# Five fences between the stages of an encoder block, and the place of the merge's buffers

## The chip, the cores and the metric

The kernel runs on all 8 cores of one Trainium2 chip. Each core computes one element of the batch by itself; there is no exchange between cores. The metric is the device time of the slowest core, in microseconds (us).

TensorE multiplies matrices into PSUM (8 banks of 128 x 512 f32), VectorE (DVE), ScalarE (ACT) and GpSimd (POOL) read and write SBUF, and SyncE (SP) and GpSimd issue the loads. Each engine runs its own instructions in order and waits for the others by semaphores.

## The reference, cut to what matters

One layer on x of 2048 tokens x 1024 channels (each core's share), with f32 inputs:

```
x = x + 0.5 * swiglu(rmsnorm(x), ...)                  # D_FF = 2816
h = rmsnorm(x)
proj = h @ w_in        # q, k, v of NA | q (2 maps), k (2 maps), v of diff | q of memory
y_na   = neighbourhood_attention(...) @ w_br_na        # 8 heads of 64, window 8 x 16 on a 32 x 64 grid
y_diff = rmsnorm(differential_attention(...)) @ w_br_diff   # 4 heads, softmax1 - lam * softmax2
y_mem  = memory_attention(...) @ w_br_mem              # 4 heads of 128, 256 memory tokens
g = sigmoid(h @ w_gate + b_gate)                       # one gate per branch and channel
x = x + (g0 * y_na + g1 * y_diff + g2 * y_mem) @ w_out
x = x + 0.5 * swiglu(rmsnorm(x), ...)
return rmsnorm(x)
```

The change lies in the middle part, from the memory attention to the last merge.

## The kernel before

x stays in SBUF for the whole program (xs), the normed and transposed h too (hT, bf16). All else shares one region R of 108 KB per partition, cut by hand into overlapping views; SB = 55296 is where the attention stages' part begins. The middle part runs in this order:

1. **Memory attention**, four heads. Per head: load_win brings the q slice of w_in, proj_fm multiplies it with hT (L569, 32 matmuls in four chunks of 512 tokens, two PSUM banks in turn, each emptied by ScalarE), then scores, exp, values, and transposes (L591) into oT, the stage's output.
2. **Merge 0** (merge, L617). Eight column steps c. Per step: the 128 columns of w_br and w_gate are loaded into one of two slots (wbrs, wgts), and for each of four chunks n there are 4 matmuls of oT with w_br (L634), 8 of hT with w_gate (L639), a sigmoid on ScalarE (L648) into sig, and on VectorE the product with the branch (L653; in merges 1 and 2 L657 into tt, then L659 adds it to mergedT).
3. **Neighbourhood attention**, four pairs of heads: three slices of w_in and a bias table nab, q and k projections, v projection (L733), and per token tile the scores with the bias added by a matmul (L763).
4. **Merge 1**, then **differential attention**, four heads: two score maps, with the bias (alibi) added by VectorE (L852) and exp on ScalarE (L855); each block of 512 tokens ends in a chain of ScalarE and VectorE work (L871 to L893) with two f32 matmuls inside it (L886).
5. **Merge 2**, then the output projection (L910) and the second feed-forward part.

In stages 3 and 4 q is kept in two tensors whose unused halves are zero, qT and QB. Before each of the stages VectorE clears these halves by two memsets (L715 and L716, L810 and L811); ScalarE's copies out of the projection's banks (L574, L577) write the other halves and are ordered behind the memsets.

**What sets the order.** There is no scheduler. The program is recorded as a list of operations with keys that they read and write; each engine runs its own in that order, and Prog.emit turns the dependences into semaphore waits. A wait on a load is a wait on its stream (a semaphore for each buffer), and asks for all loads that were issued on that stream so far in the program:

```
def stream_value_before(stream, idx):
    v = 0
    for (i, c) in stream_hist[stream]:
        if i < idx:
            v = c
```

So the second load on a stream waits for the first if it writes a key whose last writer is a load of the same stream (w_gate behind w_br in a step; the three slices of w_in from a slot's second use on).

**The fence.** Prog.fence (L61) takes the last operation of each engine and of each stream; the next operation recorded on each engine waits for all of them:

```
snap = set(self.last_of_eng.values()) | set(self.last_of_stream.values())
for e in ENGINES:
    self.pending[e] = set(snap) | self.pending.get(e, set())
```

A fence stands ahead of each merge and one behind it (L705, L713, L797, L804, L899, L901). They protect memory that is used under two names: the merge's wbrs, wgts and sigs lie over qT, kT and vaug of the attention stages, its tts over the exp tiles Et.

**Prefetch.** merge takes a function after_first, called when the loads of step 0 have been recorded: pre_na and pre_df load the w_in slices and the table of the next stage's first head. load_win takes its slot from a counter, alternating between 0 and 1 (wsl, two slots of three slices at SB+12416 and SB+18560). All loads but alibi, mem, params, gfin and x are issued by GpSimd (L353, L710, L722).

Of the kernel before, what the change touches and what calls it, by code (L numbers as in the profile page):

```python
# [6 lines left out]
F32 = mybir.dt.float32  # L7
BF16 = mybir.dt.bfloat16
AF = mybir.ActivationFunctionType
ALU = mybir.AluOpType  # L10
# [4 lines left out]
KD = 8  # L15
# [278 lines left out]
def build_nc():  # L294
# [180 lines left out]
    SB = 55296  # L475
# [131 lines left out]

    wctr = [0]

    def load_win(cols):  # L610
        s = wctr[0] % 2
        wctr[0] += 1
        for i, c0 in enumerate(cols):
            wload(wsl[s][i], win_d[:, c0:c0 + 128], ("wsl", s, i), "wsl%d" % s)
        return s

    def merge(bi, wbr, first, after_first=None):  # L617
        wbrs = [rv(SB + i * 1024, 1024, BF16, "p (k n) -> p k n", k=4) for i in range(2)]
        wgts = [rv(SB + 2048 + i * 2048, 2048, BF16, "p (k n) -> p k n", k=KD) for i in range(2)]
        sigs = [rv(SB + 6144 + i * 2048, 2048, F32) for i in range(2)]  # L620
        tts = [rv(SB + 24704 + i * 2048, 2048, F32) for i in range(2)]
        gidx = {0: 2, 1: 0, 2: 1}[bi]
        ev = 0
        for c in range(KD):
# [5 lines left out]
            for n in range(4):  # L630
                py, pyk = poolA.next()
                pg, pgk = poolB.next()
                for k in range(4):
                    P.add("pe", lambda e, k=k, py=py, sl=sl, n=n: e.matmul(  # L634
                        py, lhsT=wbrs[sl][:, k, :], rhs=oT[:, k, n * 512:(n + 1) * 512],
                        start=(k == 0), stop=(k == 3)),
                        reads=[("wbr", sl), ("oT", k, n)], writes=[pyk])
                for k in range(KD):
                    P.add("pe", lambda e, k=k, pg=pg, sl=sl, n=n: e.matmul(  # L639
                        pg, lhsT=wgts[sl][:, k, :], rhs=hT[:, k, n * 512:(n + 1) * 512],  # L640
                        start=(k == 0), stop=(k == KD - 1)),
                        reads=[("wgt", sl)] + [("hT", t) for t in range(4 * n, 4 * n + 4)], writes=[pgk])
                sg = sigs[ev % 2]
                tt = tts[ev % 2]
                sgk, ttk = ("sig", ev % 2), ("tt", ev % 2)
                ev += 1
                bcol = 32 + gidx * 8 + c
                P.add("act", lambda e, sg=sg, pg=pg, bcol=bcol: e.activation(  # L648
                    out=sg, in_=pg, func=AF.Sigmoid, bias=par[:, bcol:bcol + 1]),
                    reads=["par"], writes=[sgk, pgk])  # L650
                mslice = mergedT[:, c, n * 512:(n + 1) * 512]
                if first:
                    P.add("dve", lambda e, sg=sg, py=py, mslice=mslice: e.tensor_tensor(  # L653
                        out=mslice, in0=py, in1=sg, op=ALU.mult),
                        reads=[sgk], writes=[("mT", c, n), pyk])
                else:
                    P.add("dve", lambda e, sg=sg, py=py, tt=tt: e.tensor_tensor(  # L657
                        out=tt, in0=py, in1=sg, op=ALU.mult), reads=[sgk], writes=[ttk, pyk])
                    P.add("dve", lambda e, tt=tt, mslice=mslice: e.tensor_tensor(  # L659
                        out=mslice, in0=tt, in1=mslice, op=ALU.add), reads=[ttk], writes=[("mT", c, n)])  # L660

    for h in range(4):
        s = load_win([O_MQ + h * 128])
        proj_fm(qT, O_MQ + h * 128, wsl[s][0], ("wsl", s, 0), 128.0 ** -0.5)
        units = []
        for n in range(4):
# [35 lines left out]
            transposes_to_oT(h, n, otokb, [("otokb", j) for j in range(4)])  # L702

        pipeline(units, stage_a, stage_b, 1)
    P.fence()  # L705
    na_pre = {}

    def pre_na():
        na_pre[0] = (load_win([O_NQ, O_NK, O_NV]), True)
        P.dma("pool", lambda e: e.dma_start(out=nabt, in_=nab_d[0:2].rearrange("h v k q -> k h v q")),  # L710
              writes=["nabt"], stream="nab")
    merge(0, wbr_d[0], True, after_first=pre_na)
    P.fence()  # L713
    vaugn = vaug[:, :, 0:130].rearrange("p t (h c) -> p t h c", h=2)
    P.add("dve", lambda e: e.memset(qT[64:128, :], 0.0), writes=[("qT", n) for n in range(4)])  # L715
    P.add("dve", lambda e: e.memset(QB[0:64, :], 0.0), writes=[("qT", n) for n in range(4)])  # L716
    for hp in range(4):
        if hp in na_pre:
            s = na_pre[hp][0]
        else:  # L720
            s = load_win([O_NQ + hp * 128, O_NK + hp * 128, O_NV + hp * 128])
            P.dma("pool", lambda e, hp=hp: e.dma_start(  # L722
                out=nabt, in_=nab_d[2 * hp:2 * hp + 2].rearrange("h v k q -> k h v q")),
                writes=["nabt"], stream="nab")
# [69 lines left out]
                    transposes_to_oT(hp, t // 4, otokb, [("otokb", j) for j in range(4)])  # L794

        pipeline(units, stage_a, stage_b, 1)
    P.fence()  # L797
    df_pre = {}

    def pre_df():  # L800
        df_pre[0] = load_win([O_DQ, O_DK, O_DV])
        P.dma("sp", lambda e: e.dma_start(out=alib, in_=alibi_d[0]), writes=["alib"], stream="alibi")
    merge(1, wbr_d[1], False, after_first=pre_df)
    P.fence()  # L804
    vt = vaug[:, :, 0:128]
    tA = rv(SB + 28800, 2048, F32)
    tB = rv(SB + 50816, 2048, F32)
# [11 lines left out]
    for h in range(4):  # L819
        if h in df_pre:  # L820
            s = df_pre[h]
        else:
            s = load_win([O_DQ + h * 128, O_DK + h * 128, O_DV + h * 128])
            P.dma("sp", lambda e, h=h: e.dma_start(out=alib, in_=alibi_d[h]), writes=["alib"], stream="alibi")
        proj_fm(qT, 0, wsl[s][0], ("wsl", s, 0), 0.125, split=True)
        proj_fm(kT, 0, wsl[s][1], ("wsl", s, 1), 1.0)
# [69 lines left out]
                    reads=["tA", "tB", "sublnc"], writes=[("oT", h, n)])  # L896

        pipeline(units, stage_a, stage_b, 2, with_index=True)
    P.fence()  # L899
    merge(2, wbr_d[2], False)  # L900
    P.fence()  # L901

# [79 lines left out]
```

How the kernel before makes its waits and increments, by code:

```python
            def run(engname, eng):  # L209
                for op in per_eng[engname]:
                    wl = waits_of[op.idx]
                    attach = None
                    if ATTACH_WAIT and wl and not op.is_dma:
                        attach = wl[-1]
                        wl = wl[:-1]
                    for key, val in wl:
                        sem = st_sem[key[1]] if key[0] == "d" else eng_sem[key[1]]
                        eng.wait_ge(sem, val)
                    ins = op.fn(eng)
                    if attach is not None:
                        key, val = attach
                        sem = st_sem[key[1]] if key[0] == "d" else eng_sem[key[1]]
                        ins._wait_ge(sem, val)
                    if op.is_dma:
                        ins.then_inc(st_sem[op.stream], 16)
                    elif op.signal:
                        ins.then_inc(eng_sem[op.eng], 1)
                if engname == "sp":
                    for s in final_wait_streams:
                        eng.wait_ge(st_sem[s], stream_count[s])
```

## Time and profile before

| what | us |
|---|---|
| median of three runs | 2421.61 |
| fastest and slowest of them | 2420.55, 2474.15 |
| the profiled execution | 2421.05 |
| its span on core 1, the slowest | 2418.1 |
| spans of the other cores | 2407.3 to 2416.6 |

The span runs from the first to the last instruction of a core; some 3 us of the execution's time lie outside it. On core 1 the memory stage runs from 583 to 677 us, merge 0 to 779, neighbourhood attention to 985, merge 1 to 1093, differential attention to 1715 and merge 2 to 1811. The two feed-forward parts lie before and behind.

In the timeline, "x8" is a run of eight instructions of one kind, and the bracket at the end is the idle time of that engine just before, with what ended it. A matmul's own duration (0.38 us for 512 columns) includes its way through the array; the distance between starts tells the rate. The granted clock is a share of 2.4 GHz: 1.00 is that level, 0.50 is 1.2 GHz, and values between them are means over a stretch. "issue" is time in which an engine waited for nothing that the profile shows.

### The profile page before, as it was taken

How to read it: one execution, taken by the hardware profiler on the slowest of the kernel's cores; microseconds unless marked ns; L12 is line 12 of the kernel's file. 1: busy time of each engine (PE TensorE's matmuls, PEld its weight loads, DVE VectorE, ACT ScalarE, POOL GpSimd, SP SyncE). 2: the span in 40 equal slices, each digit the busy share in tenths (PEclk: the TensorE clock that was granted, in tenths of full speed). 3: DMA queues.
4: the chain of work that ended last, by engine and by line, in shares of the span. 5: the costliest groups of instructions: out<-in, count | busy, mean ns of one | idle time of the engine just before them, and what ended most of it. 6: DMA issues, size and time to landing. Idle time of an engine off the chain costs nothing.

```text
span 2418.1 us, 27123 instructions; the slowest of 8 cores (2407.3 to 2418.1 us)
## 1 busy us (share of the span) xinstructions
PE 2051.3 (85%) x11424; PEld 952.7 (39%) x11424; DVE 983.0 (41%) x1576; ACT 900.2 (37%) x1526; POOL 120.2 (5%) x140
## 2 busy tenths in 40 slices
PE   1999999995869999598888787887797499999995
PEld 0444444443334677343233232232243244444442
DVE  1332323363223122255747757567452314232327
ACT  5301111162322656325766767667322310101013
POOL 1000000000011010110000000000110010000000
PEclk9999999996779999899889898898898699999998
DMA  9323221004063342432010000000222352322103
GB/s 220 46 35 44 35 36 18 1 1 66 5 62 33 36 46 25 67 33 27 0 39 9 0 34 1 34 1 0 26 27 35 52 79 27 45 35 35 18 1 148
DMA packets 148776, 89.54 MB, mean 37 GB/s; under 512 B 89776, under 2 KB 137008, under 8 KB 148144
## 3 DMA queue, kind: packets, MB, share of 16 engines
q0 software_dynamic: 143104, 61.12, 21.4%
q1 hardware_dynamic: 5552, 26.70, 3.2%
q8 instruction: 89, 1.46, 0.2%
q14 instruction: 31, 0.25, 0.0%
HBM read 140.54 MB, written 8.39 MB: 62 GB/s over the span
## 4 chain that ended last, share of the span: by engine, by line
PE 72%; DVE 12%; ACT 9%; DMA 6%; issue 1%; POOL 0%; SPq 0%; DVEq 0%; POOLq 0%; ACTq 0%
PE B L453 13%; PE B L432 13%; PE B L437 13%; PE B L639 7%; PE B L569 6%; DVE R L852 5%; ACT R L855 5%; PE B L634 4%; PE B L862 3%; PE B L910 2%; DVE hT L395 2%; DMA xs<-x 2%; PE B L845 2%; PE B L865 2%; DMA R<-w_in 1%
## 5 line engine op out<-in xcount | busy, mean ns | idle before, releaser
L444 ACT ACTIVATE R<-B 128x512 f32<-128x512 f32 x176 | 105.1, 597 | 777.5 <-PE B L432 777.5
L855 ACT ACTIVATE R<-R 128x512 bf16<-128x512 f32 x512 | 321.4, 630 | 109.6 <-DVE R L852 103.9
L432 PE MATMUL B<-hT,R 128*128 128x512 bf16 x1408 | 334.3, 380 | 27.1 <-DMA R<-ffn_w_up 27.1
L852 DVE TENSOR_TENSOR R<-B,R 128x512 f32<-128x512 f32 x512 | 337.9, 690 | 46.7 <-PE B L845 46.7
L437 PE MATMUL B<-hT,R 128*128 128x512 bf16 x1408 | 332.9, 379 | 0.0
L446 DVE TENSOR_TENSOR R<-B,R 128x512 bf16<-128x512 f32 x176 | 121.7, 691 | 513.1 <-PE B L437 513.1
L453 PE MATMUL B<-R 128*128 128x512 bf16 x1408 | 310.3, 379 | 0.0
L862 PE MATMUL B<-R 128*128 128x512 bf16 x512 | 202.3, 395 | 36.7 <-ACT R L855 26.2
L457 DVE SCALAR_TENSOR_TENSOR xs<-B,xs 128x512 f32<-128x512 f32 x256 | 177.0, 691 | 132.5 <-PE B L453 129.6
L432 PEld LDWEIGHTS B<-hT,R 128*128 128x128 bf16 x1408 | 138.0, 98 | 193.8 <-issue 28.9
L437 PEld LDWEIGHTS B<-hT,R 128*128 128x128 bf16 x1408 | 137.9, 98 | 166.6 <-issue 0.8
L453 PEld LDWEIGHTS B<-R 128*128 128x128 bf16 x1408 | 134.5, 98 | 174.4 <-DVE xs L457 22.7
L845 PE MATMUL B<-R 128*128 128x512 bf16 x512 | 200.5, 394 | 0.0
L865 PE MATMUL B<-R 128*128 128x512 bf16 x512 | 199.2, 389 | 0.0
L639 PE MATMUL B<-hT,R 128*128 128x512 bf16 x768 | 185.4, 385 | 0.0
L569 PE MATMUL B<-hT,R 128*128 128x512 bf16 x640 | 153.9, 404 | 14.8 <-DMA R<-w_in 6.4
L648 ACT ACTIVATE R<-B,par 128x512 f32<-128x512 f32 x96 | 66.0, 687 | 236.0 <-PE B L639 236.0
L634 PE MATMUL B<-R 128*128 128x512 bf16 x384 | 101.2, 387 | 50.4 <-DMA R<-w_in 39.5
L862 PEld LDWEIGHTS B<-R 128*128 128x128 bf16 x512 | 50.3, 98 | 233.6 <-ACT R L855 221.4
L639 PEld LDWEIGHTS B<-hT,R 128*128 128x128 bf16 x768 | 76.3, 99 | 94.1 <-issue 6.0
L569 PEld LDWEIGHTS B<-hT,R 128*128 128x128 bf16 x640 | 65.4, 103 | 102.5 <-issue 25.9
L392 PE MATMUL B<-identb,R 128*128 128x128 bf16 x384 | 46.1, 295 | 68.1 <-ACT R L387 61.0
(111 smaller groups left out, 1761.4 us busy)
## 6 DMA issues: line engine op xcount, KB each, us to landing
R<-ffn_w_gate POOLq DMA_DIRECT2D x22, 512.0 KB, 5.9
R<-ffn_w_up POOLq DMA_DIRECT2D x22, 512.0 KB, 5.7
R<-ffn_w_down POOLq DMA_DIRECT2D x6, 1536.0 KB, 13.1
xs<-x SPq DMA_DIRECT2D x4, 2048.0 KB, 30.0
y<-R SPq DMA_DIRECT2D x16, 512.0 KB, 3.4
R<-alibi SPq DMA_DIRECT2D x4, 1984.0 KB, 7.9
R<-w_in POOLq DMA_DIRECT2D x28, 256.0 KB, 4.7
R<-w_gate POOLq DMA_DIRECT2D x24, 256.0 KB, 4.4
```

What stands on the lines that cost most here:

```text
L432: P.add("pe", lambda e, k=k, pg=pg, sl=sl, cc=cc, n=n: e.matmul(pg, lhsT=wgs[sl][:, k, cc * 128:(cc + 1) * 128], rhs=hT[:, k, n * 512:(n + ...
L437: P.add("pe", lambda e, k=k, pu=pu, sl=sl, cc=cc, n=n: e.matmul(pu, lhsT=wus[sl][:, k, cc * 128:(cc + 1) * 128], rhs=hT[:, k, n * 512:(n + ...
L453: P.add("pe", lambda e, c=c, po=po, t=t, j=j, wd=wd, ncg=ncg: e.matmul(po, lhsT=actT[:, c, t * 128:(t + 1) * 128], rhs=wd[:, c, j * 512:(j ...
L457: P.add("dve", lambda e, po=po, t=t, j=j: e.scalar_tensor_tensor(out=xs[:, t, j * 512:(j + 1) * 512], in0=po, scalar=0.5, in1=xs[:, t, j * ...
L569: P.add("pe", lambda e, k=k, n=n, pb=pb: e.matmul(pb, lhsT=slot_ap[:, k, :], rhs=hT[:, k, n * 512:(n + 1) * 512], start=(k == 0), stop=(k ...
L634: P.add("pe", lambda e, k=k, py=py, sl=sl, n=n: e.matmul(py, lhsT=wbrs[sl][:, k, :], rhs=oT[:, k, n * 512:(n + 1) * 512], start=(k == 0), ...
L639: P.add("pe", lambda e, k=k, pg=pg, sl=sl, n=n: e.matmul(pg, lhsT=wgts[sl][:, k, :], rhs=hT[:, k, n * 512:(n + 1) * 512], start=(k == 0), ...
L845: P.add("pe", lambda e, m=m, kt=kt, n=n, pb=pb: e.matmul(pb, lhsT=kT[:, kt * 128:(kt + 1) * 128], rhs=QAB[m][:, n * 512:(n + 1) * 512], st ...
L852: P.add("dve", lambda e, sp_=sp_, pb=pb, off=off: e.tensor_tensor(out=sp_, in0=pb, in1=alib[:, off:off + 512], op=ALU.add), reads=["alib"] ...
L855: P.add("act", lambda e, sp_=sp_, E=E: e.activation(out=E, in_=sp_, func=AF.Exp), reads=[spk], writes=[ek])
L862: P.add("pe", lambda e, E=E, kt=kt, ob=ob: e.matmul(ob, lhsT=vt[:, kt, :], rhs=E, start=(kt == 0), stop=(kt == NT - 1)), reads=[ek, ("v", ...
L865: P.add("pe", lambda e, E=E, kt=kt, sb=sb: e.matmul(sb, lhsT=onesb, rhs=E, start=(kt == 0), stop=(kt == NT - 1)), reads=[ek, "onesb"], wri ...
```

## The change

Five of the six fences go; the one behind merge 2 (L901) stays. So that the merges can run without them,

- the merge's w_br and w_gate buffers move from SB and SB+2048 to SB+18560 and SB+20608. That is w_in's slot 1, and load_win now gets force=0 everywhere, so that all slices go to slot 0;
- the sigmoid's output goes to the two buffers spr, which otherwise only differential attention uses (key "spr");
- tt stays on the exp tiles, and its operations now name the keys of the tiles it covers ("E");
- the alibi prefetch names nabt too, over which it lies.

```diff
--- before.py
+++ after.py
@@ -607,17 +607,17 @@
 
     wctr = [0]
 
-    def load_win(cols):
-        s = wctr[0] % 2
+    def load_win(cols, force=None):
+        s = wctr[0] % 2 if force is None else force
         wctr[0] += 1
         for i, c0 in enumerate(cols):
             wload(wsl[s][i], win_d[:, c0:c0 + 128], ("wsl", s, i), "wsl%d" % s)
         return s
 
     def merge(bi, wbr, first, after_first=None):
-        wbrs = [rv(SB + i * 1024, 1024, BF16, "p (k n) -> p k n", k=4) for i in range(2)]
-        wgts = [rv(SB + 2048 + i * 2048, 2048, BF16, "p (k n) -> p k n", k=KD) for i in range(2)]
-        sigs = [rv(SB + 6144 + i * 2048, 2048, F32) for i in range(2)]
+        wbrs = [rv(SB + 18560 + i * 1024, 1024, BF16, "p (k n) -> p k n", k=4) for i in range(2)]
+        wgts = [rv(SB + 20608 + i * 2048, 2048, BF16, "p (k n) -> p k n", k=KD) for i in range(2)]
+        sigs = [spr[i] for i in range(2)]
         tts = [rv(SB + 24704 + i * 2048, 2048, F32) for i in range(2)]
         gidx = {0: 2, 1: 0, 2: 1}[bi]
         ev = 0
@@ -642,7 +642,8 @@
                         reads=[("wgt", sl)] + [("hT", t) for t in range(4 * n, 4 * n + 4)], writes=[pgk])
                 sg = sigs[ev % 2]
                 tt = tts[ev % 2]
-                sgk, ttk = ("sig", ev % 2), ("tt", ev % 2)
+                sgk, ttk = ("spr", ev % 2), ("tt", ev % 2)
+                tal = [("E", 2 * (ev % 2)), ("E", 2 * (ev % 2) + 1)]
                 ev += 1
                 bcol = 32 + gidx * 8 + c
                 P.add("act", lambda e, sg=sg, pg=pg, bcol=bcol: e.activation(
@@ -655,12 +656,12 @@
                         reads=[sgk], writes=[("mT", c, n), pyk])
                 else:
                     P.add("dve", lambda e, sg=sg, py=py, tt=tt: e.tensor_tensor(
-                        out=tt, in0=py, in1=sg, op=ALU.mult), reads=[sgk], writes=[ttk, pyk])
+                        out=tt, in0=py, in1=sg, op=ALU.mult), reads=[sgk], writes=[ttk, pyk] + tal)
                     P.add("dve", lambda e, tt=tt, mslice=mslice: e.tensor_tensor(
-                        out=mslice, in0=tt, in1=mslice, op=ALU.add), reads=[ttk], writes=[("mT", c, n)])
+                        out=mslice, in0=tt, in1=mslice, op=ALU.add), reads=[ttk] + tal, writes=[("mT", c, n)])
 
     for h in range(4):
-        s = load_win([O_MQ + h * 128])
+        s = load_win([O_MQ + h * 128], force=0)
         proj_fm(qT, O_MQ + h * 128, wsl[s][0], ("wsl", s, 0), 128.0 ** -0.5)
         units = []
         for n in range(4):
@@ -702,15 +703,13 @@
             transposes_to_oT(h, n, otokb, [("otokb", j) for j in range(4)])
 
         pipeline(units, stage_a, stage_b, 1)
-    P.fence()
     na_pre = {}
 
     def pre_na():
-        na_pre[0] = (load_win([O_NQ, O_NK, O_NV]), True)
+        na_pre[0] = (load_win([O_NQ, O_NK, O_NV], force=0), True)
         P.dma("pool", lambda e: e.dma_start(out=nabt, in_=nab_d[0:2].rearrange("h v k q -> k h v q")),
               writes=["nabt"], stream="nab")
     merge(0, wbr_d[0], True, after_first=pre_na)
-    P.fence()
     vaugn = vaug[:, :, 0:130].rearrange("p t (h c) -> p t h c", h=2)
     P.add("dve", lambda e: e.memset(qT[64:128, :], 0.0), writes=[("qT", n) for n in range(4)])
     P.add("dve", lambda e: e.memset(QB[0:64, :], 0.0), writes=[("qT", n) for n in range(4)])
@@ -718,7 +717,7 @@
         if hp in na_pre:
             s = na_pre[hp][0]
         else:
-            s = load_win([O_NQ + hp * 128, O_NK + hp * 128, O_NV + hp * 128])
+            s = load_win([O_NQ + hp * 128, O_NK + hp * 128, O_NV + hp * 128], force=0)
             P.dma("pool", lambda e, hp=hp: e.dma_start(
                 out=nabt, in_=nab_d[2 * hp:2 * hp + 2].rearrange("h v k q -> k h v q")),
                 writes=["nabt"], stream="nab")
@@ -794,14 +793,12 @@
                     transposes_to_oT(hp, t // 4, otokb, [("otokb", j) for j in range(4)])
 
         pipeline(units, stage_a, stage_b, 1)
-    P.fence()
     df_pre = {}
 
     def pre_df():
-        df_pre[0] = load_win([O_DQ, O_DK, O_DV])
-        P.dma("sp", lambda e: e.dma_start(out=alib, in_=alibi_d[0]), writes=["alib"], stream="alibi")
+        df_pre[0] = load_win([O_DQ, O_DK, O_DV], force=0)
+        P.dma("sp", lambda e: e.dma_start(out=alib, in_=alibi_d[0]), writes=["alib", "nabt"], stream="alibi")
     merge(1, wbr_d[1], False, after_first=pre_df)
-    P.fence()
     vt = vaug[:, :, 0:128]
     tA = rv(SB + 28800, 2048, F32)
     tB = rv(SB + 50816, 2048, F32)
@@ -820,7 +817,7 @@
         if h in df_pre:
             s = df_pre[h]
         else:
-            s = load_win([O_DQ + h * 128, O_DK + h * 128, O_DV + h * 128])
+            s = load_win([O_DQ + h * 128, O_DK + h * 128, O_DV + h * 128], force=0)
             P.dma("sp", lambda e, h=h: e.dma_start(out=alib, in_=alibi_d[h]), writes=["alib"], stream="alibi")
         proj_fm(qT, 0, wsl[s][0], ("wsl", s, 0), 0.125, split=True)
         proj_fm(kT, 0, wsl[s][1], ("wsl", s, 1), 1.0)
@@ -896,7 +893,6 @@
                     reads=["tA", "tB", "sublnc"], writes=[("oT", h, n)])
 
         pipeline(units, stage_a, stage_b, 2, with_index=True)
-    P.fence()
     merge(2, wbr_d[2], False)
     P.fence()
```

The instructions stand in the same order on each engine as before; what differs is what they wait for. Two places show it. The rows give the line, the instruction, what it writes and reads, and the semaphores it waits for: s_pe, s_act and s_dve are the engines, d_14 and d_15 before are the streams of w_in's slots 0 and 1, d_16 and d_18 those of the merge's two slots (d_15 and d_17 after, where slot 1 has no stream). Numbers of lines below L644 move by one to four.

GpSimd's loads at the end of the memory stage and the start of merge 0, before:

```order
L353 DMA R<-w_in 128x8x128 [waits s_pe] x2
L353 DMA R<-w_br_mem 128x4x128 [waits s_act]
L353 DMA R<-w_gate 128x8x128
L353 DMA R<-w_in 128x8x128 x3
L710 DMA R<-nab 128x42x128
```

and after:

```order
L353 DMA R<-w_in 128x8x128 [waits s_pe] x3
L353 DMA R<-w_br_mem 128x4x128
L353 DMA R<-w_gate 128x8x128
L353 DMA R<-w_in 128x8x128 [waits s_pe]
L353 DMA R<-w_in 128x8x128 x2
L710 DMA R<-nab 128x42x128
```

The first w_br no longer waits for ScalarE's last copy of the stage; the w_in slices of the next stage wait for TensorE's projection of the last head, because they now go to the slot that this projection reads; and of the memory heads' own slices three instead of two wait for TensorE.

TensorE at the end of the neighbourhood stage and the start of merge 1, before:

```order
L778 MATMUL B<-R 128x65 x3
L591 MATMUL B<-identb,R 128x128
L591 MATMUL B<-identb,R 128x128 [waits s_dve] x3
L634 MATMUL B<-R 128x512 [waits d_16,d_14]
L634 MATMUL B<-R 128x512 x3
L639 MATMUL B<-hT,R 128x512 x8
```

and after:

```order
L777 MATMUL B<-R 128x65 x3
L591 MATMUL B<-identb,R 128x128
L591 MATMUL B<-identb,R 128x128 [waits s_dve] x3
L634 MATMUL B<-R 128x512 [waits d_15]
L634 MATMUL B<-R 128x512 x3
L639 MATMUL B<-hT,R 128x512 x8
```

The first matmul of the merge has lost its wait on the stream of the w_in slices (d_14) and keeps that on its own weights.

## Rows read from the trace of the kernel before

**Rows 1.** The page: busy time and share of the span, by engine.

```profile
PE 2051.3 (85%) x11424; PEld 952.7 (39%) x11424; DVE 983.0 (41%) x1576; ACT 900.2 (37%) x1526; POOL 120.2 (5%) x140
```

**Rows 2.** TensorE's waits, longest first: line, waited for, us in all, times, longest.

```profile
PE B L634 <- DMA R<-w_in: 39.5, 2, 22.3
...
PE B L910 <- DMA R<-w_out: 17.5, 1, 17.5
...
PE B L634 <- DMA R<-w_gate: 10.8, 1, 10.8
```

**Rows 3.** Timeline at A (start us, us, engine, line, [idle before]); the last row is core 0's.

```profile
677.03 0.29 PE L591 MATMUL B<-identb,R 128*128 128x128 bf16 x1 [0.17 <-DVE R L699]
...
694.52 1.89 PE L634 MATMUL B<-R 128*128 128x512 bf16 x4 [17.20 <-DMA R<-w_in]
...
698.74 1.03 PE L634 MATMUL B<-R 128*128 128x512 bf16 x4
...
684.67 1.89 PE L634 MATMUL B<-R 128*128 128x512 bf16 x4 [12.01 <-DMA R<-w_in]
```

**Rows 4.** Timeline at B.

```profile
781.14 3.61 PE L569 MATMUL B<-hT,R 128*128 128x512 bf16 x16 [1.95 <-DVE R L653]
781.47 1.76 DVE L715 MEMSET R<- 64x2048 bf16 x1 [0.48 <-issue]
...
785.52 0.59 ACT L574 ACTIVATE R<-B 64x512 bf16<-64x512 f32 x1 [5.25 <-DVE R L716]
...
786.79 10.53 PE L569 MATMUL B<-hT,R 128*128 128x512 bf16 x48 [2.04 <-ACT R L577]
```

**Rows 5.** Timeline at C.

```profile
984.75 0.23 PE L591 MATMUL B<-identb,R 128*128 128x128 bf16 x1 [0.49 <-DVE R L788]
...
1007.30 1.89 PE L634 MATMUL B<-R 128*128 128x512 bf16 x4 [22.32 <-DMA R<-w_in]
...
1012.13 1.03 PE L634 MATMUL B<-R 128*128 128x512 bf16 x4
...
1014.72 1.03 PE L634 MATMUL B<-R 128*128 128x512 bf16 x4
```

**Rows 6.** Timeline at D.

```profile
1094.97 3.61 PE L569 MATMUL B<-hT,R 128*128 128x512 bf16 x16 [2.38 <-DVE R L659]
...
1100.62 12.19 PE L569 MATMUL B<-hT,R 128*128 128x512 bf16 x48 [2.04 <-ACT R L577]
```

**Rows 7.** Timeline at E.

```profile
1710.57 2.08 PE L886 MATMUL B<-R 128*128 128x512 f32 x2 [3.98 <-ACT R L884]
...
1714.07 0.75 DVE L893 SCALAR_TENSOR_TENSOR R<-R,stat 128x512 bf16<-128x512 f32 x1 [4.21 <-ACT R L891]
...
1723.48 1.89 PE L634 MATMUL B<-R 128*128 128x512 bf16 x4 [10.84 <-DMA R<-w_gate]
...
1728.57 1.07 PE L634 MATMUL B<-R 128*128 128x512 bf16 x4
```

**Rows 8.** Timeline of GpSimd's load issues; last, core 5's chain, issue to landing.

```profile
615.63 0.87 POOL L353 DMA_DIRECT2D R<-w_in  x1 [21.13 <-PE B L676]
...
680.13 2.64 POOL L353 DMA_DIRECT2D R<-w_in  x3
682.72 2.06 POOL L710 DMA_DIRECT2D R<-nab  x1
684.72 0.81 POOL L353 DMA_DIRECT2D R<-w_br_mem  x1
...
679.73 19.59 DMA R<-w_gate
```

**Rows 9.** Chain in the memory stage (start, us); last, a window: TensorE's busy, then clock.

```profile
630.48 8.22 PE B L569 x32
652.52 9.14 PE B L569 x32
...
673.00:677.00 4.00, 2.78 (x15) 1.42 (x15) 2.95 (x13) 0.60 (x1) 0.00 (x0) 0.50 0.00 0
```

**Rows 10.** Chain in the neighbourhood stage.

```profile
797.33 7.15 PE B L733 x128
833.64 13.81 PE B L569 x64
```

**Rows 11.** Timeline of TensorE behind one L886.

```profile
1184.37 2.08 PE L886 MATMUL B<-R 128*128 128x512 f32 x2 [5.28 <-ACT R L884]
...
1186.24 0.63 PE L845 MATMUL B<-R 128*128 128x512 bf16 x1
...
1188.80 0.63 PE L845 MATMUL B<-R 128*128 128x512 bf16 x1
```

**Rows 12.** The page's DMA issues: KB each, median us from issue to landing.

```profile
R<-w_in POOLq DMA_DIRECT2D x28, 256.0 KB, 4.7
```

**Rows 13.** The cores: span and mean granted clock.

```profile
core 0: 2407.3 us, clock 0.933
core 1: 2418.1 us, clock 0.930
```

## The prediction

> **What bounds the kernel now.** I began with the page's busy shares: TensorE is busy for 85% of the span, VectorE and ScalarE near 40% [rows 1]. So time is won where TensorE stands still, and the next view is the list of its waits [rows 2]. Two of its long entries belong to L634, the first matmul of a merge: 39.5 us in two waits on a w_in load, 10.8 us in one wait on a w_gate load. The 17.5 us on w_out sit behind a fence that stays, so they stay.
>
> The timelines then show the five boundaries between an attention stage and a merge. I call them A to E in order of time. **A**, memory attention to merge 0: TensorE's last transpose starts at 677.03 and the first matmul of the merge at 694.52, after 17.20 idle [rows 3]. **B**, merge 0 to neighbourhood attention: TensorE starts the q projection after 1.95 idle, runs 16 matmuls (two PSUM banks), and stands again for 2.04 until 786.79 [rows 4]. **C**, neighbourhood attention to merge 1: 22.32 idle [rows 5]. **D**, merge 1 to differential attention: 2.38 and 2.04 idle [rows 6]. **E**, differential attention to merge 2: 10.84 idle [rows 7].
>
> **Why A and C are so long.** A fence makes each engine's next operation wait for the last operation of every engine and of every load stream, and for a stream the emitter asks for everything issued on it so far. The prefetch of three w_in slices stands ahead of the merge's first matmul in the program, so this matmul waits for slices that only the next stage reads (it waits on d_14 beside d_16 in the order before, and on d_15 alone after). And the weights of the merge are issued only behind the fence.
>
> **The change, part by part.** No engine gets another order and no work is added. Five fences go, and three buffers find a place that is free earlier, so waits on data are what is left.
>
> *A.* The w_br and w_gate of the first column step are issued right behind the w_in of memory head 3, whose fellow for head 3 was issued long before the stage's end even now [rows 8], and the merge's banks and sig buffers are free. TensorE goes on at 677.3: +17.2. Today the merge starts at 1.2 GHz: its first 12 matmuls take 694.52 to 698.74, 4.22 us [rows 3], against 2.59 at 2.4 GHz (1012.13 to 1014.72 [rows 5]), 1.6 lost. After the change it follows a tail that the granted clock of 0.50 already marks as slow [rows 9]. The nearest rows for a dense start behind such a tail are the head projections, 8.17 and 9.14 us [rows 9], where 32 matmuls take 6.9 at full clock (half of 13.81 [rows 10]): 1.3 to 2.2 lost. Clock term 0; bounds -0.6 and +1.6.
>
> The cover here is the next load. GpSimd now issues three w_in, the nab table and the second step's w_br and w_gate as soon as head 3's projection is over (652.52 + 9.14 = 661.7 [rows 9]). It needs 5.5 us up to the start of the last issue (2.64 + 2.06 + 0.81 [rows 8]), so that starts at 667.2. Core 5 shows the worst landing of this very load behind the nab table, 19.59 us from its issue [rows 8], which gives 686.8. The merge needs it after four chunks, 677.3 + 4 x 2.59 + 1.6 = 689.3. That is 2.5 us of cover; were it gone, each us late costs one. Low end for A 14, high end 18.8.
>
> *B.* Here the fence is not what ends the stall. The third bank of the q projection needs ScalarE's copies, and these need two VectorE memsets of the unused halves of q [rows 4]. Both stand behind the merge's last VectorE operation. TensorE will start its two banks 1.95 us earlier and then wait longer in one piece, about 3.6 us. Only VectorE's 0.48 ahead of the first memset shrinks, since the memset loses its semaphore wait: +0.45. Against that: today TensorE runs on at full clock at 786.79 (48 matmuls in 10.53). The nearest rows for a single longer stretch are the 16 stops ahead of L886: after the 5.28 at 1184.37 the next seven matmuls start 0.43 apart instead of 0.22 [rows 11], 7 x 0.21 = 1.5 lost. I take -1.5 because 3.6 is nearer to these than to 2.04. B: -1.1, bounds -2.5 (12 slow matmuls) and +0.45.
>
> *C.* Loads of steps 0 and 1, the w_in slices and their serial waits now fall inside the last head's attention, at whose end GpSimd has nothing left to do. TensorE follows on at 985.0: +22.3. Today's restart is slow, 4.83 us for 12 matmuls (1007.30 to 1012.13 [rows 5]) against 2.59, and the new one has only 0.49 us of idle ahead of it: +2.2. C: 24.6, low end 22.3. The alibi load (SyncE's queue) now waits for the last reader of the nab table and has the whole merge as cover.
>
> *D.* As B: +0.45. The restart at 1100.62 is slow already (48 matmuls in 12.19, 1.7 more than at B [rows 6]), so nothing is lost: +0.15. D: +0.6, bounds -0.4 and +2.1.
>
> *E.* TensorE's L886 of the last block stands ahead of the merge in its order and waits for the softmax tail, so the merge cannot start before 1712.65 (1710.57 + 2.08 [rows 7]). From there the fence and two serial loads cost 10.84, all of which goes: the output that arrives last (0.75 us of VectorE work from 1714.07 [rows 7]) is read only in the fourth chunk, 7.8 us in. Today 12 slow matmuls follow (1723.48 to 1728.57, 2.5 lost); then the pattern behind L886, 1.5 lost. E: +11.8, bounds 10.3 and 13.3.
>
> *One slot for w_in.* Now head h+1's slices are loaded only once head h's projections have read theirs. That costs nothing while attention covers the chain: memory heads have 14 us (615.6 to 630.48 [rows 8, 9]) for one load of 4.7 us [rows 12], neighbourhood heads 29 us (804.5, the end of the v projection, to 833.64 [rows 10]) for the rest of a chain of three.
>
> **Sum.** 17.2 - 1.1 + 24.6 + 0.6 + 11.8 = 53.1. The profiled execution took 2421.05 us (span 2418.1 and 2.95 around it), 0.6 below the shown median of 2421.61. 2421.05 - 53.1 = **2368**. The slowest core is the one I summed; core 0, 11 us shorter [rows 13], loses such a wait too (12.01 at A [rows 3], where core 1 has 17.20), so its end comes to some 5 us before core 1's and does not set the time. Low ends together: 14 - 2.5 + 22.3 - 0.4 + 10.3 = 43.7, 2377. High ends: 18.8 + 0.45 + 24.6 + 2.1 + 13.3 = 59.2, 2362.
>
> **Rivals.**
> 1. *The half clock takes a part back* (0.11). Every boundary restarts slow, and the longer single stops at B and D act as those ahead of L886: B -2.5, D -0.4, E 10.3, A -0.6. Sum 17.2 - 0.6 - 2.5 + 24.6 - 0.4 + 10.3 = 48.6: 2372. For it: rows 9 and 11. Against: the restart at 786.79 ran at full clock. The Trainium skill, "TensorE: Matmul & The Clock Gate", section "HAM oscillation — how this bites in real kernels", says that gaps in TensorE's work bring the clock down to half and are paid at each restart; by that rule B's one long stop costs what two short ones did not, and the trace agrees as far as L886 goes (0.43 against 0.22 between starts).
> 2. *The second step's weights land late at A or C* (0.12). The prefetch shares the queues with the nab table on all eight cores at once. If it needs 5 to 10 us more than core 5's 19.6, A keeps 3 to 8 us of stall: 2371 to 2376, say 2375. Against: core 5's 19.6 was taken with the same loads bunched as closely on all cores, behind the fence.
> 3. *The change does little* (0.03). Waits on data take the place of the fences at A, C and E as they do at B and D; about 2415. Against: the new waits name only streams that were issued 10 to 100 us earlier.
> 4. *Slower: the single slot* (0.02). The place is the first projection of each later head. If the chain of three slices came behind attention instead of inside it, six heads would pay 3 x 4.7 = 14.1 and three memory heads 4.7, 99 us: 2368 + 99 = 2467. It decides only if a load is issued later than 5 us before the stage ends; rows 8 and 9 leave 9 us even in the shortest stage.
> 5. *More than the sum* (0.06). All restarts at full clock: 2361 or less.
>
> **Numbers.** Forecast 2368 with 0.66, its own range 2362 to 2375. The range of 2361 to 2378 adds rivals 1 and 2 and the low ends. Two per cent, about what a measurement of this kernel can tell from no change, lies at 2373.2, only 5 us above the forecast. Faster by over 2%: 0.93 x 0.66 + 0.75 x 0.11 + 0.25 x 0.12 + 0.06 = 0.79. Slower 0.02, within 2% the rest, 0.19.
>
> **What would show it.** Right: no wait of L634 on w_in; less than 1 us idle ahead of the first L634 of merges 0 and 1; that of merge 2 right behind L886; the third bank of the projections at B and D still held by ScalarE behind two memsets, with about 3.6 us idle in one piece. Wrong: a wait of L634 on w_gate in the second column step of merge 0 (rival 2); starts 0.43 apart for more than 12 matmuls behind B or E (rival 1); L569 waiting on w_in ahead of a later head (rival 4).

## The result, and the profile after

The changed kernel takes 2368.52 us (median of ten runs) where the kernel before takes 2421.16 beside it: a ratio of 0.9801, with a 95% interval of 0.9767 to 0.9835. The forecast was 2368 with a range of 2361 to 2378. The gain is 2%, so it lies just where "faster by over 2%" and "within 2%" meet, and the interval leaves both open; a later series of the same kernel gave 0.9766 (0.9742 to 0.9790). Some executions of every kernel here ran with one die at a lower clock and took longer; ratios and intervals leave them out, and the times that I compare are those of the profiled executions, none of which is one.

The profiled execution takes 2368.84 us, 52.2 less than the 2421.05 before; its slowest core is now core 5, with a span of 2367.3. First the page's busy line, which answers to [rows 1]:

```profile
PE 2047.5 (86%) x11424; PEld 950.8 (40%) x11424; DVE 982.9 (42%) x1576; ACT 901.8 (38%) x1526; POOL 120.3 (5%) x140
```

The work is the same to within 4 us on every engine. What went is idle time. TensorE's waits, which answer to [rows 2]:

```profile
PE B L906 <- DMA R<-w_out: 19.8, 1, 19.8
...
PE B L569 <- ACT R L577: 8.7, 2, 4.6
PE B L569 <- DMA R<-w_in: 5.9, 1, 5.9
```

L634 no longer stands in this list at all, neither on w_in nor on w_gate, on any of the eight cores. The w_out wait stays, as its fence does. And one row has grown: L569's wait for ScalarE's copies is 8.7 us in two pieces, where each of the two was 2.04 [rows 4, 6].

The timeline at A and at C, which answers to [rows 3, 5]:

```profile
672.97 0.29 PE L591 MATMUL B<-identb,R 128*128 128x128 bf16 x1 [0.17 <-DVE R L700]
673.06 1.91 PE L634 MATMUL B<-R 128*128 128x512 bf16 x4
...
677.47 1.03 PE L634 MATMUL B<-R 128*128 128x512 bf16 x4
...
965.24 0.23 PE L591 MATMUL B<-identb,R 128*128 128x128 bf16 x1 [0.49 <-DVE R L787]
965.31 1.03 PE L634 MATMUL B<-R 128*128 128x512 bf16 x4
...
967.90 1.03 PE L634 MATMUL B<-R 128*128 128x512 bf16 x4
```

The merge's first matmul starts within 0.1 us of the last transpose. Behind A its first 12 matmuls are slow (4.41 us), behind C they are not (2.59). At E, which answers to [rows 7]:

```profile
1668.87 2.07 PE L883 MATMUL B<-R 128*128 128x512 f32 x2 [3.98 <-ACT R L881]
1670.73 1.91 PE L634 MATMUL B<-R 128*128 128x512 bf16 x4
...
1674.65 1.03 PE L634 MATMUL B<-R 128*128 128x512 bf16 x4
```

The merge follows the last f32 matmul directly, and its first 12 matmuls take 3.92 us. At B and D, which answers to [rows 4, 6]:

```profile
757.75 3.62 PE L569 MATMUL B<-hT,R 128*128 128x512 bf16 x16
...
760.21 1.76 DVE L714 MEMSET R<- 64x2048 bf16 x1 [0.48 <-issue]
...
765.53 12.18 PE L569 MATMUL B<-hT,R 128*128 128x512 bf16 x48 [4.16 <-ACT R L577]
...
1048.19 3.62 PE L569 MATMUL B<-hT,R 128*128 128x512 bf16 x16
...
1056.39 13.50 PE L569 MATMUL B<-hT,R 128*128 128x512 bf16 x48 [4.59 <-ACT R L577]
```

TensorE starts its two banks at once, stands still in one piece (4.16 and 4.59 us), and restarts slowly at both places: 12.18 and 13.50 us for 48 matmuls that take 10.53 at full clock [rows 4]. The 13.50 is not typical: core 7 has 13.49, the four other cores with a row of 48 there have 11.84 to 11.89.

GpSimd's loads at the end of the memory stage, which answers to [rows 8]:

```profile
658.11 2.63 POOL L353 DMA_DIRECT2D R<-w_in  x3 [20.20 <-PE B L569]
660.71 2.05 POOL L710 DMA_DIRECT2D R<-nab  x1
662.71 0.80 POOL L353 DMA_DIRECT2D R<-w_br_mem  x1
663.45 0.94 POOL L353 DMA_DIRECT2D R<-w_gate  x1
```

The prefetch begins 15 us before the merge and not behind a fence.

### The profile page after: what moved, and what is told of

The parts are those of the page before. It is cut to its first block, busy times and chain, and to the rows that moved or that the text cites. A ratio compares the mean times of both kernels' runs of the same rounds, so it can differ in the third digit from the quotient of the medians.

```text
span 2367.3 us, 27129 instructions; the slowest of 8 cores (2357.2 to 2367.3 us)
## 1 busy us (share of the span) xinstructions
PE 2047.5 (86%) x11424; PEld 950.8 (40%) x11424; DVE 982.9 (42%) x1576; ACT 901.8 (38%) x1526; POOL 120.3 (5%) x140
## 4 chain that ended last, share of the span: by engine, by line
PE 73%; DVE 12%; ACT 9%; DMA 4%; issue 1%; SPq 0%; DVEq 0%; POOL 0%; POOLq 0%; ACTq 0%
PE B L453 13%; PE B L432 13%; PE B L437 13%; PE B L639 7%; PE B L569 6%; DVE R L849 5%; ACT R L852 5%; PE B L634 4%; PE B L859 3%; PE B L906 2%; DVE hT L395 2%; DMA xs<-x 2%; PE B L842 2%; PE B L862 2%; PE B L883 1%; PE B L758 1%
## 5 line engine op out<-in xcount | busy, mean ns | idle before, releaser
L453 PE MATMUL B<-R 128*128 128x512 bf16 x1408 | 310.2, 379 | 0.0
L859 PE MATMUL B<-R 128*128 128x512 bf16 x512 | 201.9, 394 | 38.0 <-ACT R L852 36.0
L842 PE MATMUL B<-R 128*128 128x512 bf16 x512 | 200.2, 394 | 0.0
L862 PE MATMUL B<-R 128*128 128x512 bf16 x512 | 199.0, 389 | 0.0
L569 PE MATMUL B<-hT,R 128*128 128x512 bf16 x640 | 157.9, 412 | 14.7 <-ACT R L577 8.7
L569 PEld LDWEIGHTS B<-hT,R 128*128 128x128 bf16 x640 | 66.5, 105 | 105.0 <-issue 26.2
L767 ACT ACTIVATE R<-B 128x512 bf16<-128x512 f32 x224 | 89.7, 459 | 36.4 <-PE B L762 34.1
```

Of the source, the lines that this page charges most:

```text
L453: P.add("pe", lambda e, c=c, po=po, t=t, j=j, wd=wd, ncg=ncg: e.matmul(po, lhsT=actT[:, c, t * 128:(t + 1) * 128], rhs=wd[:, c, j * 512:(j ...
L569: P.add("pe", lambda e, k=k, n=n, pb=pb: e.matmul(pb, lhsT=slot_ap[:, k, :], rhs=hT[:, k, n * 512:(n + 1) * 512], start=(k == 0), stop=(k ...
L842: P.add("pe", lambda e, m=m, kt=kt, n=n, pb=pb: e.matmul(pb, lhsT=kT[:, kt * 128:(kt + 1) * 128], rhs=QAB[m][:, n * 512:(n + 1) * 512], st ...
L859: P.add("pe", lambda e, E=E, kt=kt, ob=ob: e.matmul(ob, lhsT=vt[:, kt, :], rhs=E, start=(kt == 0), stop=(kt == NT - 1)), reads=[ek, ("v", ...
L862: P.add("pe", lambda e, E=E, kt=kt, sb=sb: e.matmul(sb, lhsT=onesb, rhs=E, start=(kt == 0), stop=(kt == NT - 1)), reads=[ek, "onesb"], wri ...
```

## The experiments

Each ran on all eight cores. The time is that of the profiled execution, the ratio is to the kernel before on the same chip.

| run | edit | us | ratio | 95% interval |
|---|---|---|---|---|
| e1_fences_b_d | change + fences B, D | 2365.36 | 0.9749 | 0.9727 to 0.9771 |
| e2_fence_c | change + fence C | 2394.71 | 0.9887 | 0.9836 to 0.9939 |
| e3_prefetch_later | before, prefetch in step 1 | 2416.01 | 0.9965 | 0.9950 to 0.9980 |
| e4_memsets_early | change, memsets early | 2355.77 | 0.9734 | 0.9693 to 0.9776 |
| e6_fence_a | change + fence A | 2387.49 | 0.9864 | 0.9838 to 0.9891 |
| e7_fence_e | change + fence E | 2381.33 | 0.9829 | 0.9807 to 0.9852 |
| e5_memsets_and_wout | e4, w_out in pieces, last fence gone | 2335.99 | 0.9641 | 0.9606 to 0.9676 |
| e8_prefetch_last_step | before, prefetch in step 7 | 2405.92 | 0.9913 | 0.9879 to 0.9948 |
| e9_change_again | the change | 2367.34 | 0.9766 | 0.9742 to 0.9790 |
| e10_fences_b_d_again | as e1 | 2364.46 | 0.9758 | 0.9737 to 0.9779 |

### One fence at a time: A, C, E

```diff
@@ e6 @@
+    P.fence()
     na_pre = {}
@@ e2 @@
+    P.fence()
     df_pre = {}
@@ e7 @@
+    P.fence()
     merge(2, wbr_d[2], False)
```

> The changed kernel with only the fence ahead of merge 0 put back (A). My theory: 17.2 us of idle time return on the cores that wait for all of the bunched loads, 12 to 15 on the others: 2382 to 2386 us. Rival: the merge's weights were not the point, the nab table and the slices now load before the fence ends and little is left to wait for: under 2376 us.

> The changed kernel with only the fence ahead of merge 1 put back (C). My theory: the idle time ahead of the first L634 of merge 1 returns at 22 us with a slow restart, 24.7 in all, whatever the other boundaries do: 2393 us. Rival: the savings overlap, part of C's gain came from a later stage that started elsewhere, and less than 20 us come back: under 2388 us.

> The changed kernel with only the fence ahead of merge 2 put back (E). My theory: 10.8 us of idle time and about 1.3 us of slow clock return, 12.1 us: 2381 us. Rival: ScalarE's tail and its table load for the sigmoid bound the merge's start anyway, and half of it or less returns: 2374 us or less.

Against the changed kernel's 2368.84 the fence at A costs 18.7 us, that at C 25.9, that at E 12.5. The waits of L634, one fence for each kernel (A, C, E; a row that A has beside its first is the second):

```profile
PE B L634 <- DMA R<-w_in: 17.8, 1, 17.8
...
PE B L634 <- DMA R<-w_gate: 3.4, 1, 3.4
```

```profile
PE B L634 <- DMA R<-w_in: 25.2, 1, 25.2
```

```profile
PE B L634 <- DMA R<-w_gate: 10.9, 1, 10.9
```

Each brings back the wait that stood at its place before (17.20, 22.32 and 10.84 [rows 3, 5, 7]), and no other boundary's. All three rivals fall: A's would have had under 2376 us, C's under 2388, E's 2374 or less. The three costs add up to 57.1, against the 52.2 that the whole change gained; the two fences at B and D account for 3.5 of the difference (next section). No run has all five fences on the changed kernel, so this adds up separate runs, taken on different chips. Beside C's run the kernel before took about 2426 and not 2421, and the other execution in its ratio took 2403.2, so 25.9 is good to a few us; the wait itself, 25.2, was 21.7 to 24.6 on the other cores. A came out 1.5 above the end of my range: the wait at the first matmul is there, and the one on w_gate in the second column step is on top of it on this core, 3.4 us (0.7 to 2.3 on four others, none on three). That is the late load of rival 2. The kernel before has a second, smaller wait on w_gate too on five of its cores (the longest 2.9 us), the change on none.

### The fences at B and D

```diff
     merge(0, wbr_d[0], True, after_first=pre_na)
+    P.fence()
...
     merge(1, wbr_d[1], False, after_first=pre_df)
+    P.fence()
```

> The changed kernel with the two fences behind merges 0 and 1 put back (boundaries B and D). My theory: the third bank of the q projection waits for ScalarE's copies behind two VectorE memsets, with the fence or without it, so these two fences cost nothing; the idle time splits again into 1.95 + 2.04 at B and 2.38 + 2.04 at D, the restart of B may be at full clock again, and the time is 2366 to 2369 us. Rival: a fence is worth the idle time that stood at it, so 4.0 + 4.4 come back and the time is 2377 us.

With the fences back the kernel is not slower but a little faster: 2365.36. The timeline of TensorE on its slowest core, B and D:

```profile
766.97 3.61 PE L569 MATMUL B<-hT,R 128*128 128x512 bf16 x16 [2.04 <-DVE R L654]
772.52 10.53 PE L569 MATMUL B<-hT,R 128*128 128x512 bf16 x48 [1.93 <-ACT R L577]
...
1055.97 5.21 PE L569 MATMUL B<-hT,R 128*128 128x512 bf16 x16 [2.38 <-DVE R L660]
1061.62 10.53 PE L569 MATMUL B<-hT,R 128*128 128x512 bf16 x48 [0.45 <-ACT R L577]
```

The idle time at B splits as before, 2.04 and 1.93, and the restart is at full clock. At D the two banks behind the first stop ran slowly here (5.21 us instead of 3.61), in time that would have been idle anyway, and the 48 matmuls that count ran at full clock. So where the slow stretch falls decides whether it costs. Two short stops do not always end this way, though. In the kernel before they are as long as here, and two of its eight cores restart slow at B; core 2, with one record of the 48 missing:

```profile
780.94 12.22 PE L569 MATMUL B<-hT,R 128*128 128x512 bf16 x47 [2.04 <-ACT R L577]
```

I ran both kernels again on one chip to see whether it was luck:

> The changed kernel itself, beside the next run on the same chip. Both theories: 2366 to 2369 us, with idle stretches of 4.15 and 4.6 us at B and D and 48 matmuls in 11.8 to 13.5 us behind each.

> The changed kernel with the fences behind merges 0 and 1 put back, once more, for a comparison with the changed kernel on the same chip. My theory: the fences split one long stop of TensorE into two short ones at the same end, TensorE then restarts at full clock (48 matmuls in 10.53 us at both places on every core), and the kernel with the two fences is 2 to 4 us faster than the one without them: 2363 to 2366 us. Rival: the clock at the restart is chance, the earlier run was luck, and the two differ by less than 1 us.

Without the fences every row of 48 that the traces of the change hold, in both executions, reads 11.84 to 13.50 us, and the rows of 47 (a record is missing) are slow too. With them it is 10.53 at B on every core, in both executions, and at D on seven of eight cores in each (core 2 has 47 matmuls in 11.99, then 48 in 12.22). So much is shown: one stop of 4.1 us or more was followed by the slow clock at all 32 places. The reverse is not. In the kernel before, whose stops are the same two short ones, the restart is slow on cores 2 and 4 at B and on cores 0, 1, 5 and 7 at D (12.19 to 12.22), and at D of the two runs with fences the slow stretch is not absent but lies in the 16 matmuls between the stops on the seven fast cores. What decides where it falls after short stops stays open, and my theory's "at both places on every core" was missed by one core. The kernel's own time settles less. 2364.46 against 2367.34, and 2365.36 against 2368.84, are both 3 us in favour of the fences, where the rows of the slowest cores add up to 3.6 and 5.0; over the executions in the ratios, on the common chip, the middle values are 2366.3 and 2368.8, but the single times lie among each other and the intervals of the ratios (0.9758 and 0.9766) overlap almost wholly. The gain from putting the two fences back is shown in the rows and not in the times.

### What the stop at B and D waits for

```diff
     def pre_na():
+        P.add("dve", lambda e: e.memset(qT[64:128, :], 0.0), writes=[("qT", n) for n in range(4)])
+        P.add("dve", lambda e: e.memset(QB[0:64, :], 0.0), writes=[("qT", n) for n in range(4)])
...
-    P.add("dve", lambda e: e.memset(qT[64:128, :], 0.0), writes=[("qT", n) for n in range(4)])
-    P.add("dve", lambda e: e.memset(QB[0:64, :], 0.0), writes=[("qT", n) for n in range(4)])
     for hp in range(4):
...
-    P.add("dve", lambda e: e.memset(qT[64:128, :], 0.0), writes=[("qT", n) for n in range(4)])
-    P.add("dve", lambda e: e.memset(QB[0:64, :], 0.0), writes=[("qT", n) for n in range(4)])
     P.add("dve", lambda e: e.memset(onesf, 1.0), writes=["onesf"])
```

> The changed kernel with the two memsets of stage 3 recorded in merge 0, ahead of its first product, and those of stage 4 left out (the halves are still zero from stage 3, since the merge's buffers no longer lie on them). My theory: the memsets are what holds the third bank at B and D, so 4.2 + 4.6 us of idle time and the slow restarts behind them (48 matmuls in 12.2 and 13.5 us against 10.5) go, 12 to 13 us: 2356 us. Rival: ScalarE's last sigmoids and copies hold the bank anyway, and less than 4 us are won: 2365 us or more.

2355.77, 13.1 us less than the change, as expected; but the two other executions in its ratio took 2362.99 and 2366.74, and the ratio's interval overlaps that of the run with the fences at B and D. The time alone does not decide between theory and rival, the rows do. TensorE on its slowest core, B and D:

```profile
764.54 13.98 PE L569 MATMUL B<-hT,R 128*128 128x512 bf16 x64
...
1048.92 13.98 PE L569 MATMUL B<-hT,R 128*128 128x512 bf16 x64
```

The 64 matmuls of both projections run in one piece, without a stop and at full clock. On all eight cores L569's waits for ScalarE are gone. What stood at B and D was the memsets; ScalarE's sigmoids were not in the way. By the rows this is 6.0 us at B and 7.7 at D against the change (19.96 and 21.70 us on its core 5, from the first of the 64 matmuls to the end of the last), 13.7 in all.

### Why the fences at A and C cost so much

Here the edit is to the kernel before, with all its fences.

```diff
@@ e3 @@
-            if c == 0 and after_first is not None:
+            if c == 1 and after_first is not None:
@@ e8 @@
-            if c == 0 and after_first is not None:
+            if c == 7 and after_first is not None:
```

> The kernel before, all fences kept, with the prefetch of the next stage's slices recorded in column step 1 instead of step 0. My theory: the fence makes the merge's first matmul wait for the prefetched w_in slices because they were issued on a stream that the fence names; recorded later they are not waited for. A then waits for w_br and w_gate alone (17.2 falls to about 6.5) and C for the two serial loads as E does (22.3 falls to 10.8): 22 us less than before, 2399 us, less up to 5 us that the weights of step 2 may come late behind the nab table. Rival: the stall is the drain itself and the queue's own slowness, and A and C keep at least 15 and 20 us: 2415 us or more.

2416.01, against 2399 expected: the time is the rival's, but the rival's waits are not there. The timeline of TensorE in merges 0 and 1, on core 3, the slowest:

```profile
682.15 1.89 PE L634 MATMUL B<-R 128*128 128x512 bf16 x4 [7.47 <-DMA R<-w_gate]
...
710.78 1.87 PE L634 MATMUL B<-R 128*128 128x512 bf16 x4 [6.32 <-DMA R<-w_gate]
...
991.48 1.89 PE L634 MATMUL B<-R 128*128 128x512 bf16 x4 [10.11 <-DMA R<-w_gate]
...
1022.69 1.86 PE L634 MATMUL B<-R 128*128 128x512 bf16 x4 [8.27 <-DMA R<-w_gate]
```

The first matmul's wait fell as I had said, from 17.20 to 7.47 and from 22.32 to 10.11. New are the waits in the third column step, 6.32 and 8.27 us, each with a slow restart. GpSimd's issues in merge 1 show why:

```profile
993.76 0.89 POOL L353 DMA_DIRECT2D R<-w_in  x1
1000.80 0.87 POOL L353 DMA_DIRECT2D R<-w_in  x1 [6.15 <-DMA R<-w_in]
1006.03 0.87 POOL L353 DMA_DIRECT2D R<-w_in  x1 [4.36 <-DMA R<-w_in]
1006.89 0.76 POOL L353 DMA_DIRECT2D R<-w_br_na  x1
1012.79 0.88 POOL L353 DMA_DIRECT2D R<-w_gate  x1 [5.14 <-PE B L634]
```

GpSimd issues its loads in the program's order, and each of the three slices waits for the one before, so the third step's weights stand behind 13 us of slices. I had allowed 5 us for that, at A alone. With nothing behind the slices that the merge needs the bill should stay paid:

> The kernel before, all fences kept, with the prefetch of the next stage's slices recorded in the merge's last column step instead of the first. The run with the prefetch in step 1 took the w_in wait away from the merge's first matmul (17.2 to 7.5 us at A, 22.3 to 10.1 at C) and had two thirds of it come back as waits of L634 on w_gate in step 2, since step 2's weights stood behind the slices in GpSimd's order. My theory: in the last step nothing stands behind the slices that the merge needs, and the stage's own first use is 20 us away, so both waits stay gone and nothing comes back: 22 us less than before, 0.991 of it, 2399 us by the first runs. Rival: the slices and the nab table now come late for the projection of the next stage, L569 waits on w_in, and less than 14 us are won: 2407 us or more.

2405.92; beside the kernel before, 0.9913, some 21 us less by that ratio. The waits of this kernel:

```profile
PE B L634 <- DMA R<-w_gate: 26.9, 3, 11.0
...
PE B L569 <- DMA R<-alibi: 6.7, 1, 6.7
PE B L569 <- DMA R<-nab: 5.4, 1, 5.4
```

Nothing is late inside the merges; their three first waits on w_gate are left. But the fence behind the merge now makes the projection wait for nab and alibi, which it does not read, by the same rule that made the merge wait for w_in. So an edit of one digit gives about 0.9% with all fences kept (0.5 to 1.2% by the interval), and the rest came with the fences gone. The ratio is the one that I had forecast, 0.991. The absolute 2399 was too low, as it was counted from the 2421 of the first runs, while the kernel before takes about 2424 beside this one; it lies nearer to the rival's 2407. The rival's wait on w_in did not appear, but it was half right: the nab table does come late.

### The version that beats both

```diff
+    wout = rv(SB, 16384, BF16, "p (k n) -> p k n", k=KD)
+    def load_wout(c):
+        P.dma("pool", lambda e, c=c: e.dma_start(out=wout[:, c, :], in_=wout_d[c * 128:(c + 1) * 128, :]),
+              writes=[("wout", c)] + [(q, i) for q in ("qT", "kT", "v") for i in range(4)]
+              + [("wsl", 0, i) for i in range(3)], stream="wout%d" % c)
-    merge(2, wbr_d[2], False)
-    P.fence()
+    merge(2, wbr_d[2], False, each=load_wout)    # each(c) is called behind step c's loads
-    wload(wout, wout_d[:, :], "wout", "wout")
```

> As the run with early memsets, and the last fence (behind merge 2) gone too: w_out is loaded in eight pieces, one in each column step of merge 2, into the space of q, k, v and slot 0, which is free by then. My theory: the wait for w_out (17.5 us before, 19.8 in the changed kernel) and the slow restart behind it (about 2 us) go: 2336 us, and 3.5% less than the kernel before. Rival: the pieces delay the merge's own weights in the shared queue, L634 waits on w_gate in merge 2, and less than 12 us are won: 2344 us or more.

2335.99, ratio 0.9641 (0.9606 to 0.9676), as expected, and 2334.39 and 2337.47 in the two other executions in its ratio. The group of the output projection, from the lines view:

```profile
L908 PE MATMUL B<-R 128*128 128x512 bf16 x256 | 55.4, 379 | 0.0
```

Its 256 matmuls have no idle time before them, where the change has 19.8 us, and each takes 379 ns. L634 has no wait on w_gate in this kernel, so the pieces of w_out hold nothing up.

## Why the prediction was right, point by point

The measured terms, all from the rows shown, taken as idle time plus what the slow clock adds to the matmuls behind it (at A, C and E: from the last instruction before the boundary to the start of the merge's second chunk):

| place | before | after | gain | predicted |
|---|---|---|---|---|
| A | 677.03 to 698.74, 21.7 | 672.97 to 677.47, 4.5 | 17.2 | 17.2 |
| B | 1.95 + 2.04 + 0 | 4.16 + 1.65 | -1.8 | -1.1 |
| C | 984.75 to 1012.13, 27.4 | 965.24 to 967.90, 2.7 | 24.7 | 24.6 |
| D | 2.38 + 2.04 + 1.66 | 4.59 + 2.97 | -1.5 | +0.6 |
| E | 1710.57 to 1728.57, 18.0 | 1668.87 to 1674.65, 5.8 | 12.2 | 11.8 |
| sum | | | 50.8 | 53.1 |

The rows of before are core 1's and those of after core 5's, each the slowest. The span fell by 50.8 too (2418.1 to 2367.3), but that the two agree is chance. Core 5 reached A 4.1 us earlier after the change than core 1 before it, which is no gain of the change: the eight cores reach A within 671.3 to 677.0 before and 670.9 to 677.8 after. It lost 1.2 us between D and E and 3.1 behind E again, 2.3 of them at the wait for w_out (19.8 against 17.5). The profiled time fell by 52.2, since 1.5 us instead of 2.9 lie around the span.

**A, C, E: right, and shown.** The waits left with the fences and came back with each of them. The explanation for A and C, that the fence waits for slices nobody in the merge reads, is shown by the two prefetch runs: the wait at the first matmul shrank by 9.7 and 12.2 us with every fence in place.

**A's cover: held.** I put it at 2.5 us; no L634 of merge 0 waited on w_gate in the change, on any core. On core 5 the load was issued at 663.45 and landed 18.1 us later, at about 681.6, and the second column step began at 685.24: 3.7 us were left.

**B and D: the mechanism was right, the sizes were off.** That the memsets and not the fence end the stall is shown by the runs with the two fences back and with the memsets moved. The first mis-sized step is "+0.45, since the memset loses its semaphore wait". In the kernel before, the first memset carries a wait on the stream of nab (at D of alibi), which had been met long before; after the change it carries none, and VectorE's 0.48 ahead of it is there all the same. From this memset to the third bank it is 5.32 us before (781.47 to 786.79 [rows 4]) and 5.32 after (760.21 to 765.53), so nothing was saved, at B or at D. The second is D's "nothing is lost, the restart is slow already": on core 5 it became slower, 13.50 instead of 12.19. On four of the six cores that have the row it did not (11.84 to 11.89), so this part lies in the core that happened to be the slowest. Together they made the sum 2.8 us too high; C and E gave 0.5 back.

**The clock.** I took B's restart to be slow because its single stop was nearer to those ahead of L886 than to 2.04, and it was, on every core. By the rule of the Trainium skill, "TensorE: Matmul & The Clock Gate", section "HAM oscillation — how this bites in real kernels", that gaps in TensorE's work bring the clock to half and each restart pays, the trace agrees for the long stop: one of 4.13 to 4.16 us at B left 48 matmuls at 11.95 to 12.22. That two short ones are free I had read from core 1 alone. It held on every core with the fences put back, but in the kernel before cores 2 and 4 restart slow at B, and on these the 1.5 us that I charged were being paid already.

**The single slot: no cost.** No L569 of a later head waits on w_in; the one such wait is the first of the memory stage, 5.9 us after and 6.4 before.

**The chances.** The likeliest case came true to half a us, which is partly luck: the sum was 2.3 us too high, the time around the span came out 1.4 us shorter, and what lies outside the five places happened to cancel. The 0.11 for rival 1 leaned on core 1's restart alone. I gave 0.79 to more than 2% although the forecast lay only 5 us beyond that line, and the result lies on it.

## What to carry to other kernels

Before you price a fence, list what it waits for: here more than half of the idle time at the two dearest places was for loads of the next stage that were issued as early as possible on purpose, and moving them behind everything the stage itself needs gave 0.9% without touching a fence. Then ask of each stop what would end it if the fence were gone; at two of five places it was two memsets, which could be done a whole merge earlier or left out. And where one engine issues all loads in order, look at what stands behind a prefetch: in the run with the prefetch in step 1, merge 1's third step had to wait for 13 us of slices.

## What the runs showed of the hardware

- One stop of TensorE of 4.1 to 5.0 us was followed by the slow clock at all 32 places seen (both executions of the change, eight cores, B and D): 1.3 to 3.0 us lost where all 48 matmuls behind it are recorded. Two stops of about 2 us with 3.6 us of matmuls between them were followed by none at B on 22 of 24 cores (all 16 with the fences put back, six of eight in the kernel before). At D, with 2.38 us first, there was a slow stretch on all 16 cores with the fences put back, 14 times between the stops, and on four of eight in the kernel before. Doing part of the work earlier and then waiting in one piece cost 3.3 us on most cores, by the rows, against the two fences that did nothing else.
- VectorE's 0.48 us ahead of a memset stands between the merge's last product and the memset whether that memset carries a wait for a semaphore (already met) or not.
- A w_gate of 256 KB that is issued right behind three w_in slices and the nab table (1344 KB) lands late: 19.59 us after its issue on core 5 of the kernel before [rows 8], 15.5 to 18.6 us on the eight cores of the change, where the median of all w_gate loads is 4.4 and 4.7. That the nab table is what holds it back was not tested apart.
